# Norm inverse applied to matmul results instead of to the matmul's input, at the four joints of a second-kind stage

## The reference

```python
def rms_norm_2(x, gain):
    y = xf * lax.rsqrt(jnp.mean(xf * xf, axis=-1, keepdims=True) + RMS_EPS)
    return y.astype(x.dtype) * gain

for l in range(DEPTH):
    h = rms_norm_2(x, g_pre_mix[l])
    m = hybrid_mixer_2(h, ...)         # h @ w_in, rope, two attentions, sigmoid gates, projections, w_out
    x = x + rms_norm_2(m, g_post_mix[l])
    h = rms_norm_2(x, g_pre_ffn[l])
    f = conv_ffn(h, ...)               # u = h @ w_up; 3-tap conv per channel + bias; gelu(gate) * up; @ w_down
    x = x + rms_norm_2(f, g_post_ffn[l])
```

## Time and profile before

| | |
|---|---|
| median of three runs | 3132.31 us |
| profiled execution | 3133.0 us, its span 3131.3 us |
| TensorE clock granted, mean | 0.971 of full |
| busy: PE, DVE, ACT, POOL | 97%, 54%, 40%, 45% |
| chain that ended last | PE 88%, DVE 8%, ACT 1% |
| PE's largest wait | 19.8 us at the start, then 11.4 us in 7 joints for the reciprocal and 10.6 us in 7 joints for the first `hh` |

### The profile page before, as it was taken

The page is one execution under the profiler, slowest core; times in us unless marked ns, Lnnn a source line. Parts: engine busy times, 40 slices in busy tenths (PEclk is TensorE's granted clock), DMA queues, the critical chain, the costliest instruction groups (busy, mean ns, idle before and its releaser), DMA issues.

```text
span 3131.3 us, 40053 instructions
## 1 busy us (share of the span) xinstructions
PE 3027.1 (97%) x14910; PEld 2419.8 (77%) x14910; DVE 1685.7 (54%) x2918; ACT 1237.6 (40%) x2445; POOL 1395.7 (45%) x1196
## 2 busy tenths in 40 slices
PE   6998999999998999999999999999999999999998
PEld 5776788888776788888867688888887677888886
DVE  7786756623796554223375746554245666565521
ACT  3445432233345432233354534344334544443432
POOL 2441355545432254445542545444464335454443
PEclk9998899998999899999999999999999999999999
DMA  5422457632420122322421122323332211322222
GB/s 220 132 81 74 148 189 245 237 99 71 131 88 28 41 91 94 100 94 83 131 89 44 52 81 84 99 95 100 99 108 91 75 49 60 97 81 99 94 94 75
DMA packets 92977, 316.54 MB, mean 101 GB/s; under 512 B 12016, under 2 KB 12656, under 8 KB 92656
## 3 DMA queue, kind: packets, MB, share of 16 engines
q1 hardware_dynamic: 92784, 313.99, 30.3%
HBM read 301.36 MB, written 2.10 MB: 97 GB/s over the span
## 4 chain that ended last, share of the span: by engine, by line
PE 88%; DVE 8%; ACT 1%; issue 1%; DMA 1%; SPq 0%; POOL 0%; DVEq 0%; ACTq 0%
PE bank L199 23%; PE bank L200 23%; PE bank L201 23%; PE bank L1872 2%; PE bank L1893 2%; PE bank L1926 2%; DVE sel L1392 1%; PE bank L429 1%; DVE small L1391 1%; PE bank L430 1%; PE bank L1159 1%; PE bank L433 1%; PE bank L545 1%; DVE qk L1448 1%; PE bank L443 1%
## 5 line engine op out<-in xcount | busy, mean ns | idle before, releaser
L182 POOL TENSOR_TENSOR wl<-raw,wh 128x512 fp32r<-128x512 f32 (+1 forms) x952 | 1242.7, 1309 | 1552.9 <-ACT wh L171 1552.3
L171 ACT ACTIVATE wh<-raw 128x512 fp32r<-128x512 f32 (+1 forms) x952 | 589.0, 624 | 1361.7 <-PE bank L201 1267.7
L199 PE MATMUL bank<-hh,wh 128*128 128x512 f32 x2368 | 946.0, 399 | 5.1 <-POOL wl L182 3.8
L201 PE MATMUL bank<-hh,wl 128*128 128x512 f32 x2368 | 927.0, 391 | 0.0
L200 PE MATMUL bank<-hl,wh 128*128 128x512 f32 x2368 | 926.6, 391 | 0.0
L199 PEld LDWEIGHTS bank<-hh,wh 128*128 128x128 f32 x2368 | 446.8, 189 | 129.2 <-issue 32.9
L201 PEld LDWEIGHTS bank<-hh,wl 128*128 128x128 f32 x2368 | 447.0, 189 | 95.8
L200 PEld LDWEIGHTS bank<-hl,wh 128*128 128x128 f32 x2368 | 447.4, 189 | 89.8 <-issue 0.5
L201 PE MATMUL bank<-hidh,wl 128*128 128x512 f32 x704 | 273.9, 389 | 0.0
L199 PE MATMUL bank<-hidh,wh 128*128 128x512 f32 x704 | 273.9, 389 | 0.0
L200 PE MATMUL bank<-hidl,wh 128*128 128x512 f32 x704 | 273.9, 389 | 0.0
(11 more groups left out here) (399 smaller groups left out, 4144.4 us busy)
## 6 DMA issues: line engine op xcount, KB each, us to landing
raw<-in_w SPq DMA_DIRECT2D x444, 512.0 KB, 3.5
mod_raw2a<-in_wmod SPq DMA_DIRECT2D x28, 512.0 KB, 4.5
mod_raw2b<-in_wmod SPq DMA_DIRECT2D x28, 512.0 KB, 4.9
raw<-in_w SPq DMA_DIRECT2D x32, 384.0 KB, 3.0
first_mods<-in_wmod SPq DMA_DIRECT2D x16, 512.0 KB, 13.8
mod_raw<-in_wmod SPq DMA_DIRECT2D x12, 512.0 KB, 3.4
out_raw<-in_wmod SPq DMA_DIRECT2D x12, 512.0 KB, 4.9
tmp<-rawb SPq DMA_DIRECT2D x72, 64.0 KB, 2.3
```

What stands on the lines that cost most here:

```text
L171: act.activation(self.m.wh[:, t % 2, w_], self.m.raw[:, t % RING, w_], ACT.Copy)\
L182: pool.tensor_tensor(self.m.wl[:, t % 2, w_], self.m.raw[:, t % RING, w_], self.m.wh[:, t % 2, w_].bitcast(F32), ALU.subtract)\
L199: pe.matmul(out, wh, xh, start=start, stop=False)
L201: return pe.matmul(out, wl, xh, start=False, stop=stop)
```

## The change

A new function `plain_junction` serves the four joints. It takes y's norm as before, but the input that it hands on is x times the gain without the inverse norm: ACT makes both `hh` (L693 in the new file) and an unrounded copy in bank 6 or 7 (L696) from x, and DVE subtracts. All of y's multiplications are DVE's. The second inverse is still computed, but its spread is issued behind the paired chunks (`late_spread`), and ACT copies it into `acc` (`inverse`). It is then applied to what the products give:

- in `gate_up`, DVE multiplies each of the 44 banks in place before ACT evicts it;
- in `second_mixer`, DVE first makes `cos_n` and `sin_n` from the rotary tables; `plain` tiles are evicted by DVE with a multiplication in place of ACT's copy; merge banks are multiplied in place by DVE before ACT's tanh; values are scaled by token with `xinv4`.

```diff
+    def plain_junction(sems, product, scales, cols=None):
...
+        def gpsimd(pool):
+            pool.wait_ge(x_ready, 1)
+            for k in range(1, KD):
+                pool.wait_ge(added_ready, k + 1)
+                pool.tensor_tensor(m.x[:, k, :], m.x[:, k, :], m.y[:, k, :], ALU.add).then_inc(x_ready, 1)
...
+            for tb in range(NT):
+                ins = column(ps[4][:, 2 * tb:2 * tb + 2], m.sq[:, 1, :], tb, last_gain, stop=(tb == NT - 1))
+            ins.then_inc(sum_ready, 1)
+            for tb in range(NT):
+                column(ps[2][:, tb:tb + 1], cross_sum, tb, ones[:, 0:1], start=(tb == 0))
+            pe.wait_ge(col_ready, 1)
+            spread(pe, ps[5], inv4).then_inc(inv_ready, 1)
+            pe.wait_ge(cross_ready, KD)
+            for tb in range(NT):
+                ins = column(ps[2][:, tb:tb + 1], m.sq[:, 0, :], tb, ones[:, 0:1], stop=(tb == NT - 1))
+            ins.then_inc(sum_ready, 1)
+
+        def late_spread(pe):
+            pe.wait_ge(col_ready, 2)
+            spread(pe, ps[4], xinv4).then_inc(inv_ready, 1)
+
+        def scalar(act):
+            act.wait_ge(sum_ready, 1)
+            act.activation(root4, y_sum, ACT.Sqrt, bias=m.eps[:, 0:1], scale=1.0 / D).then_inc(root_ready, 1)
+            for k in range(KD):
+                act.wait_ge(x_ready, k + 1)
+                act.activation(m.hh[:, k, :], m.x[:, k, :], ACT.Identity, scale=scales[:, k:k + 1]).then_inc(head_ready, 1)
+                if k >= 2:
+                    act.wait_ge(h_ready, k - 1)
+                act.activation(ps[6 + k % 2][:], m.x[:, k, :], ACT.Identity, scale=scales[:, k:k + 1])\
+                   .then_inc(scaled_ready, 1)
+                if k == 5:
+                    act.wait_ge(mean_ready, 1)
+                    act.activation(xroot4, mean4, ACT.Sqrt, bias=m.eps[:, 0:1], scale=1.0 / D).then_inc(root_ready, 1)
+            act.wait_ge(inv_ready, 2)
+            act.activation(inverse, ps[4][:], ACT.Copy).then_inc(inv_copied, 1)
+
+        def vector(dve):
+            step = Signal(dve, order)
+            if cols is not None:
+                cols(dve, step)
+            dve.wait_ge(root_ready, 1)
+            dve.reciprocal(inv4, root4).then_inc(col_ready, 1)
+            dve.wait_ge(col_ready, 1)
+
+            def add(k):
+                dve.wait_ge(y_ready, k + 1)
+                dve.tensor_tensor(m.y[:, k, :], m.y[:, k, :], ps[5][:], ALU.mult).then_inc(added_ready, 1)
...
+            def rest(k):
+                dve.wait_ge(head_ready, k + 1)
+                dve.wait_ge(scaled_ready, k + 1)
+                dve.tensor_tensor(m.hl[:, k, :], ps[6 + k % 2][:], m.hh[:, k, :].bitcast(F32), ALU.subtract)\
+                   .then_inc(h_ready, 1)
...
+            dve.tensor_tensor(m.x[:, 0, :], m.x[:, 0, :], m.y[:, 0, :], ALU.add).then_inc(x_ready, 1)
+            add(1)
+            add(2)
+            rest(0)
+            add(3)
+            rest(1)
+            add(4)
+            rest(2)
+            add(5)
+            rest(3)
+            add(6)
+            rest(4)
+            add(7)
+            dve.wait_ge(sum_ready, 2)
+            step(dve.scalar_tensor_tensor(between4, cross4, 2.0, part4, ALU.mult, ALU.add))
+            step(dve.tensor_tensor(between4, between4, inv4, ALU.mult))
+            step(dve.tensor_tensor(mean4, between4, mean4, ALU.add))
+            dve.tensor_scalar(mean4, mean4, 0.0, None, ALU.max).then_inc(mean_ready, 1)
+            rest(5)
+            dve.wait_ge(root_ready, 2)
+            dve.reciprocal(xinv4, xroot4).then_inc(col_ready, 1)
+            rest(6)
+            rest(7)
+        stage = Stage(None, gpsimd, tensor, scalar, vector)
+        stage.head_ready, stage.h_ready, stage.x_ready = head_ready, h_ready, x_ready
...
         def tensor(pe):
             for c in range(KD):
                 paired_chunk(pe, t0, c, head_ready, h_ready)
+            if conv:
+                joint.late_spread(pe)
             for q in range(1, PAIRS):
                 for j in range(2):
                     if j == 0 and q >= 2:
@@ -718,7 +829,7 @@
                     bank = ps[2 * pair + j]
                     s.heads(act, t + 2, t + 3)
                     if conv:
-                        s.done(act, t)
+                        act.wait_ge(normed, 2 * q + j + 1)
                         if q >= 2:
...
+
+            def normalise(q, j, bank):
+                if q == 0 and j == 0:
+                    dve.wait_ge(joint.inv_copied, 1)
+                s.done(dve, t0 + 2 * q + j)
+                dve.tensor_tensor(bank[:], bank[:], joint.inverse, ALU.mult).then_inc(normed, 1)
 
             for q in range(PAIRS):
                 pair = q % 2
@@ -771,9 +888,11 @@
                         rope_clamp(dve, side_step, rest2, dst, quarter).then_inc(reduced, 1)
                         dve.wait_ge(reduced, 1 if q == 6 else 2)
                 if conv:
+                    normalise(q, 0, gate_bank)
                     dve.wait_ge(gate_base, q + 1)
                     step(tap(gs, pair, gate_bank, B_CW + 44 + q, 1))
                     tap(gs, pair, gate_bank, B_CW + q, 2).then_inc(gate_conv, 1)
+                    normalise(q, 1, up_bank)
                     dve.wait_ge(up_base, q + 1)
                     step(tap(us, pair, up_bank, B_CW + 44 + KF + q, 1))
                     step(tap(us, pair, up_bank, B_CW + KF + q, 2))
...
             for t in range(2, IN2):
                 kind, c = kinds[t]
+                if t == V0:
...
-                    s.done(act, t0 + t)
-                    act.activation(plain_to[kinds[t]], ps[bank_of[t]][:], ACT.Copy).then_inc(bank_free[bank_of[t]], 1)
                 if kind == "merge":
-                    s.done(act, t0 + t)
+                    act.wait_ge(inverted, c + 1)
                     if c >= 13:
                         act.wait_ge(products, 2 * 4 * NT)
                     act.activation(gm[:, c, :], ps[bank_of[t]][:], ACT.Tanh, scale=0.5)\
@@ -2060,7 +2183,7 @@
                 if kind == "svalue" and c == 3:
...
-                dve.tensor_tensor(dst, ps[bank][:], m.cos[:], ALU.mult)
-                dve.tensor_tensor(sines[r % 2][:], ps[bank][:], m.sin[:], ALU.mult).then_inc(sine_ready, 1)
+                dve.tensor_tensor(dst, ps[bank][:], cos_n[:], ALU.mult)
+                dve.tensor_tensor(sines[r % 2][:], ps[bank][:], sin_n[:], ALU.mult).then_inc(sine_ready, 1)
...
+            def plain(t):
+                s.done(dve, t0 + t)
+                bank = bank_of[t]
+                dve.tensor_tensor(plain_to[kinds[t]], ps[bank][:], joint.inverse, ALU.mult).then_inc(bank_free[bank], 1)
+
+            dve.wait_ge(joint.inv_copied, 1)
+            dve.tensor_tensor(cos_n[:], m.cos[:], joint.inverse, ALU.mult)
+            step(dve.tensor_tensor(sin_n[:], m.sin[:], joint.inverse, ALU.mult))
             for t in range(IN2):
                 kind, c = kinds[t]
+                if t and kinds[t - 1] in plain_to:
+                    plain(t - 1)
                 if t - 1 in rope_of:
                     r = rope_of[t - 1]
                     rope(r)
...
                 if (t, 0) in slots:
                     slot(slots[t, 0])
                 if t in after:
                     after[t]()
+                if kind == "merge":
+                    s.done(dve, t0 + t)
+                    bank = ps[bank_of[t]][:]
+                    dve.tensor_tensor(bank, bank, joint.inverse, ALU.mult).then_inc(inverted, 1)
                 if (t, 1) in slots:
...
-            ffs.append(gate_up(take(S, "gu_", GU_SEMS), take(S, "side_", SIDE_SEMS), gu0, mids[-1].head_ready, mids[-1].h_ready, not first,
+            mids.append(junction(mid_sems, out_sems, ff_pre) if first else plain_junction(mid_sems, out_sems, ff_pre[0]))
...
-                ends.append(junction(end_sems, dn_sems, (m.pc[:, B_PRE:B_PRE + KD], None), cols=next_cols(l)))
+                ends.append(plain_junction(end_sems, dn_sems, m.pc[:, B_PRE:B_PRE + KD], cols=next_cols(l)))
```

More of the change, by code:

```diff
@@ L661, in build, with gate_up @@
     posi2 = nc.alloc_sbuf_tensor_at("posi2", [P, T], I32, offset=tmp_at)
-    def gate_up(sems, side, t0, head_ready, h_ready, conv, side_mods=None, next_rope=False):
-        gate_base, up_base, gate_conv, gate_act, hid_ready, pair_free, order = sems
+    def gate_up(sems, side, t0, joint, conv, side_mods=None, next_rope=False):
+        gate_base, up_base, gate_conv, gate_act, hid_ready, pair_free, normed, order = sems
+        head_ready, h_ready = joint.head_ready, joint.h_ready
         c_in, c_act, mod_in0, mod_in1, mod_used, pos_in, reduced, side_order = side
@@ L1688, in second_mixer @@
          cmp_ready, gates, score, weights, turned, pv, cshift, cexp, cweights,
-         keeps, keeps_masked, betas_masked, suffixes, products, normed, feat_ready,
+         keeps, keeps_masked, betas_masked, suffixes, products, normed, feat_ready, inverted,
          order) = sems[8:]
```

(3 more changed lines are left out.)

42 lines of the change are left out of this document (33 added, 9 removed).

## The result

The changed kernel takes 3163.95 us (median of six runs, 3161.93 to 3166.84) against 3132.51: a ratio of 1.0097, 95% interval 1.0075 to 1.0119, so some 30 us slower. The direction was right, and so was the larger of the two losses that follow, in the merge tiles; the joints, forecast to gain 1.2 us, lose 10.6 here, and the time lies above the range that was given. The profiled execution has a span of 3161.6 us, 30.3 above that of before. Ratios compare undisturbed executions alone, which leaves out one single execution of all, one of e11's ten with 4989.55 us at a mean clock of 0.556.

A forecast was written before the change was run, and what follows sets the result against it. PE, busy 97% of 3131.3 us, was taken as the bound. Joints -1.2, mixers' first part +1.0 and merge tiles +18.2 gave +18.0 on 3133.0: 3151 us, range 3130 to 3162.

The forecast's parts named there:

- The joint, step by step: Four joints: PE starts 4.2 us earlier, then waits for the third tile's weights; -1.2 us in all, between -6 and +8.
- Rival 3: Clock falls in the gap ahead of each third tile: +2 us more a joint, loop stretches at half rate; 3159, chance 0.10.
- Mixer, merge tiles: Merge tiles of two mixers: tanh waiting for DVE's multiplication closes a loop that delays PE; +18.2 us, 11 to 24.
- Rival 1: Merge-tile loop stays open for the most part: a once-only lag of 3 us a mixer, without growth; 3139, chance 0.20.
- Rival 2: Joints keep PE's earlier start, third tile's weights cause no wait, merges cost nothing: -12.4 us, 3121, chance 0.12.
- Feed-forward: The 88 added DVE multiplications of banks in `gate_up`: nothing on the path, no cost.
- rival 4: Feed-forward path is late by 0.2 us a tile: +18 us again, 3169, chance 0.05.
- Mixer up to the merges: Mixer ahead of its merge tiles: two tables and nine copies moved to DVE cost +0.5 us a mixer, 0 to 2.
- `max` beside POOL: In a joint's second norm, DVE's `max` is held up by POOL's addition: 1.27 us, against 0.2 undisturbed.

The follow-up runs named there:

- e11: e5 with each merge bank's multiplication done twice in a row on DVE; 3140.7 us, ratio 1.003.
- e1: Changed kernel with ACT's copy of the second inverse moved behind the third tile's two weight heads; 3147.06 us, ratio 1.0052.
- e6: Changed kernel with 11 unused 512-column matmuls behind the late spread of each of the four joints; 3157.99 us, ratio 1.0077.
- e2: Changed kernel without the merge banks' multiplications, so the gates lack the inverse norm; 3142.15 us, ratio 1.0038.
- e5: Changed kernel with only ACT's merge-tile tanh moved behind ACT's part of the tile's second slot, DVE unchanged; 3145.05 us, ratio 1.0031.
- e10: Changed kernel, same order, with a merge tile's multiplication covering only 128 of its bank's 512 columns; 3158.22 us, ratio 1.008.
- e4: Changed kernel with the moves of e1 and e3 together; 3144.91 us, ratio 1.0045.
- e7: e1 with the multiplications and tanh of merge tiles 6 to 11 put off to merge tiles 13 to 15; 3124.04 us, ratio 0.9969.
- e8: Changed kernel with the moves of e1 and e5 together; 3124.5 us, ratio 0.9977.
- e9: e8 with 5 unused 512-column matmuls ahead of the first paired chunk of the four joints; 3121.73 us, ratio 0.9964.
- e3: Changed kernel with a merge tile's DVE multiplication and ACT tanh both moved behind the tile's second slot; 3158.65 us, ratio 1.0092.

## Why the prediction was wrong

The chains of waits held at all points of the sum; the time failed by one term, the joints.

- **The joint, step by step: the failed step.** "A joint thus gains 0.3 us", four of them -1.2, between -6 and +8; measured +10.6, and +5.0 to +11.9 in the six executions with this code. The chain was right: first paired matmul 6.9 us behind the last dense one in the first joint, where 6.9 had been worked out (1474.3 less 1467.4), and a wait for `wl` of 2.55 where 2.7 was worked out. A joint in which the clock fell no further was nearly right as well: +0.3 to +0.6 in five joints, where -0.3 had been worked out; in the first joint the difference is in the chunks (13.8 us, 13.1 worked out). Two things of the clock were missing: the stretch at 1.2 GHz behind the gap (three joints of the changed kernel; e1 and e6 show that the gap makes it), and, in the same three joints, a fall already within the column sums, which made the first window of the second joint 8.2 us instead of 6.9. The cause of the second is not known.
- **Rival 3 was therefore true together with the forecast**, at 3159, and its price of 2 us a joint was right (the table under e6: some 1.7 more with the stretch than without). I gave it a chance of 0.10 and added it only in its own case: with the gap itself in the sum, what the clock does behind it was no separate mishap. The range, too, was narrower than its terms: +8, +4 and +24 at their upper ends give 3169, where 3162 was given.
- **Mixer, merge tiles.** 18.2 expected; from slot 42 on, 10.1 in the second mixer and 11.6 in the first, 21.6 in all. The jump of the clock in the first goes with 1.5 of the difference, and most of the rest is the last wait, behind slot 51: 0.3 worked out, 1.2 measured in either mixer. The loop is shown by e2, e5 and e10. Inside it one step was wrong though its numbers fit: DVE's, of which the prediction says "its own round is about 11.9", in rows of 256. e5 and e11 show that DVE's round is not what binds there. That 8.9 stands against 8.8 after tile 11 is partly luck: tile 8 cost 1.5 us for 2.5 worked out, and tile 9 1.3 for 0.6.
- **Rival 1** (the loop stays open) fell: lateness grows tile by tile.
- **Rival 2** (the joints win) was decided by the order of ACT's instructions, as said. e1, e4, e7, e8 and e9 show its size when the order is changed: -6.5 to -8.2 for four joints, where -12.4 was worked out.
- **Small slips** that moved nothing: the parts for rows of 384 add up to 11.5, not 11.6; DVE's 8 multiplications, addition and 8 rests to 11.2, not 12; and by the 0.63 of the earlier trace rows the clock comes back some 4.2 us after the first paired matmul, not 3.9.
- **Feed-forward**: nothing, as said, so rival 4 fell. PE's lateness stays the same to 0.01 us through both `gate_up`, with 88 multiplications of 0.70 us each. **Mixer up to the merges**: +0.3 each, +0.5 expected.
- **`max` beside POOL**: 0.87 us where 1.27 was taken and 0.17 is what L628 took with POOL idle. It ended with POOL's addition, 1944.88 against 1944.86.

```profile
1943.57 1.29 POOL L660 TENSOR_TENSOR x<-x,y 128x512 f32<-128x512 f32 x1 [0.27 <-DVE y L714]
...
1944.01 0.87 DVE L743 TENSOR_SCALAR col<-col 128x4 f32<-128x4 f32 x1
```

The Trainium skill, SBUF — State Buffer, section "SBUF: two separate sides", has a DVE operation in a two-port mode and a GpSimd operation exclude each other for a whole instruction. The trace agrees, as `max` is over when POOL's addition is; whether `max` runs in such a mode no row tells. In the changed kernel no wait of PE shows for it (busy 13.76 of 13.80 us over the chunks). In e1 it begins to count: where the clock is back sooner, PE waits 0.7 and 0.6 us, in the second and fourth joint, for the `hl` that DVE makes right behind `max` (row of the second joint). What the kernels would gain without this delay was not run.

```profile
1942.55 0.73 PE L433 MATMUL bank<-hl,wh 128*128 128x512 f32 x2 [0.74 <-DVE hl L721]
```

## What to carry to other kernels

When work moves from one engine to another, list what stands behind the waiting instruction on its engine, and move that consumer back by one step: here a tanh that nobody needs soon held up sigmoids that PE needed at once, and some 20 us came back for one moved instruction. Moving producer and consumer together (e3) only moves the loop. The copy of the inverse is a second case: its values are needed late, and it had been put ahead of a weight head that was needed first. Where a new gap of PE of 2 to 3 us enters a sum, enter also the possible clock loss behind it, 1.4 to 2.1 us a time in this kernel (e6 against the changed kernel, second and fourth joint).

## What the runs showed of the chip beyond that

- A gap of 2.5 us, shortly after the joint's own slow stretch, was followed by 1.2 GHz in 18 of 24 joints; filled with matmuls of no use, in none of 4; without it, in none of 20. Why not in all 24 stays open.
- The clock also falls with PE busy. In the kernel before, PE is busy for all of the 5.1 us from 1467.4 to 1472.5, most of it with matmuls of one column, and then goes to 1.2 GHz for 10.2 us; the other three of the four joints there have 10.2 us as well. In the 48 joints of the changed kernel and its edits it is 10.2 us in 15 and 6.8 in 33, with the same column sums in all. Why it falls earlier in some of them stays open. Window of the kernel before:

```profile
1467.40:1472.50 5.10, 5.10 (x48) 5.08 (x46) 1.39 (x4) 1.96 (x4) 2.16 (x2) 1.00 0.32 108
```

- The kernel before, not changed at all, took from 3120.71 to 3152.5 us in the 24 runs that stood beside the last experiments, and the time went with the mean clock: a span of 3119.0 us at 0.976, one of 3150.8 at 0.963. Differences of 0.1% need many runs here, and the lateness of each matmul against its start before tells more than the medians do.
